# Gate and up of the first layer as seven block products per group of 512 columns

## The reference, cut to what matters

```python
def rms_norm(x, w, eps=1e-6):
    return x * lax.rsqrt(jnp.mean(x * x, axis=-1, keepdims=True) + eps) * w

for l in range(2):
    x = x + mixer[l](rms_norm(x, mix_norm_w[l])) @ w_out[l]
    h = rms_norm(x, ffn_norm_w[l])                    # 512 x 1024
    x = x + (silu(h @ w_gate[l]) * (h @ w_up[l])) @ w_down[l]   # 2816 hidden columns
return rms_norm(x, final_norm_w)
```

## Time and profile before

| | |
|---|---|
| median of the runs | 1233.5 us |
| profiled execution | 1233.71 us, of which the span is 1231.9 us |
| TensorE busy | 1218.4 us, 99% of the span |
| VectorE, ScalarE, POOL busy | 721.6, 515.9, 81.2 us |
| DMA | 122.12 MB, mean 99 GB/s |

### The profile page before, as it was taken

How to read it: one execution, slowest core, us unless ns; L and a number is a source line. 1 busy time by engine, 2 the same in 40 slices (tenths; PEclk the granted TensorE clock), 3 DMA queues, 4 the chain that set the end, 5 groups by cost and what they waited for, 6 DMA issues and landing times.

```text
span 1231.9 us, 16390 instructions
## 1 busy us (share of the span) xinstructions
PE 1218.4 (99%) x5871; PEld 985.6 (80%) x5871; DVE 721.6 (59%) x1176; ACT 515.9 (42%) x845; POOL 81.2 (7%) x179
## 2 busy tenths in 40 slices
PE   9999999999999999999999999999999999999998
PEld 7876658888888888888888888788888888888876
DVE  6787886544444443224777756645565555456796
ACT  6344455432333332123577254445333333224564
POOL 0000000000000000000001734400000000000120
PEclk9999999999999999999999999999999999999999
DMA  7232311332223333222222211011344434436781
GB/s 246 97 117 79 109 49 55 117 103 87 87 99 102 102 101 104 90 97 86 86 90 99 69 50 37 35 52 52 103 133 114 108 98 103 109 102 213 166 151 69
DMA packets 52309, 122.12 MB, mean 99 GB/s; under 512 B 21410, under 2 KB 21666, under 8 KB 52002
## 3 DMA queue, kind: packets, MB, share of 16 engines
q1 hardware_dynamic: 48754, 111.44, 28.6%
q0 software_dynamic: 2592, 8.65, 3.9%
q10 hardware_dynamic: 912, 1.35, 0.4%
HBM read 112.88 MB, written 2.10 MB: 93 GB/s over the span
## 4 chain that ended last, share of the span: by engine, by line
PE 90%; DVE 6%; ACT 2%; issue 1%; ACTq 0%; POOL 0%; DVEq 0%; POOLq 0%
PE PS L1840 89%; DVE wring L1319 1%; PE PS L1916 0%; DVE resid L1323 0%; DVE kept L1359 0%; DVE cacc L1514 0%; ACTq L979 0%; DVE wring L1369 0%; DVE amax L1432 0%; DVE AA L1363 0%; PE PS L2139 0%; ACT wring L792 0%; DVE out L1831 0%; DVE wbuf L1443 0%; DVE hbuf L1639 0%
## 5 line engine op out<-in xcount | busy, mean ns | idle before, releaser
L1840 PE MATMUL PS<-HH,wring 128*128 128x512 f32 x3096 | 723.9, 392 | 0.9 <-DVE vd L1766 0.9
L1840 PEld LDWEIGHTS PS<-HH,wring 128*128 128x128 f32 x3096 | 575.4, 188 | 118.9 <-issue 1.3
L1840 PE MATMUL PS<-AA,wring 128*128 128x512 f32 (+1 forms) x792 | 183.3, 391 | 0.4 <-DVE AA L1448 0.3
L1242 DVE TENSOR_TENSOR wring<-raw,wring 128x1024 fp32r<-128x1024 f32 x108 | 132.0, 1222 | 87.8 <-ACT wring L820 87.6
L1840 PEld LDWEIGHTS PS<-AA,wring 128*128 128x128 f32 x792 | 148.1, 188 | 32.2 <-issue 1.0
L820 ACT ACTIVATE wring<-raw 128x1024 fp32r<-128x1024 f32 x108 | 113.3, 1050 | 109.9 <-PE PS L1840 103.4
L1250 DVE TENSOR_TENSOR ubuf<-PS,rstd 128x512 f32<-128x512 f32 x44 | 30.4, 691 | 183.8 <-PE PS L1840 183.8
L1840 PE MATMUL PS<-wring,AA 128*128 128x512 f32 x462 | 105.4, 389 | 1.6 <-DVE wring L1319 0.8
L1840 PEld LDWEIGHTS PS<-wring,AA 128*128 128x128 f32 x462 | 86.6, 188 | 20.3 <-issue 2.4
L792 ACT ACTIVATE wring<-raw 128x1024 fp32r<-128x1024 f32 x67 | 70.5, 1057 | 76.4 <-PE PS L1840 58.2
L1369 DVE TENSOR_TENSOR wring<-raw,wring 128x1024 fp32r<-128x1024 f32 x67 | 82.5, 1234 | 26.4 <-ACT wring L792 26.4
(11 more groups left out here) (311 smaller groups left out, 1201.3 us busy)
## 6 DMA issues: line engine op xcount, KB each, us to landing
raw<-w_stream SPq DMA_DIRECT2D x171, 512.0 KB, 3.3
kept<-w_last POOLq DMA_DIRECT2D x10, 512.0 KB, 7.6
raw<-w_last SPq DMA_DIRECT2D x5, 512.0 KB, 3.5
kept<-w_last SPq DMA_DIRECT2D x5, 512.0 KB, 6.1
reps<-ub SPq DMA_DIRECT2D x32, 66.5 KB, 2.2
resid<-turned SPq DMA_DIRECT2D x16, 128.0 KB, 5.1
more_first<-w_last SPq DMA_DIRECT2D x1, 1536.0 KB, 12.9
more_first<-w_last POOLq DMA_DIRECT2D x3, 512.0 KB, 5.7
```

The costliest lines, as they stand in the source:

```text
L1242: V.tensor_tensor(wring[:, t % RING, 1], raw[:, t % RAW], wring[:, t % RING, 0].bitcast(f32), ALU.subtract).then_inc(lo_ready[t % RING], 1)
L1840: return nc.tensor.matmul(out, lhsT, rhs, start=start, stop=stop, skip_group_check=adds)
```

## The change

The first two chunks of 128 hidden columns stay as they were: 4 tiles, 96 matmuls (`plain_gate_up`). The other 20 chunks become five groups of 512 columns of gate and 512 of up. A group is a product of two 2x2 block matrices: tokens (two halves of 256) by depth (two halves of 512) on the left, depth by (gate, up) on the right. B11 and B21 are the gate's upper and lower half, B12 and B22 those of up. Seven block products of sums take the place of eight. A block product is 256 tokens by 512 deep by 512 wide, two tiles of 12 matmuls each.

- Left: four sums of token blocks (`diff_full`, `sum_full`, `cross_full`, and the negative of the second depth half, `left_minus`) are made once, from a float32 copy `scaled` of the weighted rows, and split into pairs.
- Right: six of the seven right sides come out of three buffers. `x` holds B11, then B11+B21 (accumulating transfer), then B11+B21+B22 (VectorE, `sum_weights`), then all four (accumulating transfer); `w` holds B21, then B21+B22 (accumulating transfer); `y` holds B22; B12 comes through `raw`. A group is thus 8 plain transfers on SP and 6 accumulating ones on POOL, each of 512 KB. In `wring` a group is 14 tiles of 12 matmuls, where it was 8 tiles of 24.
- Now the tokens are stationary and the weights the moving 512 columns. Results lie with tokens on partitions: 1/rms is a factor per partition (`rtok`), given to Silu as its scale and to VectorE's multiplications. Then TensorE transposes the group's products back, 16 transposes of 128x128 per group (`turn_results`), while the next group runs, and ScalarE copies them out (`keep_turned`).
- `AA` is gone here: the products are kept in float32 (`AF`) and split during `down` (`chunk_high`, `chunk_low`) into four places `AS`. `down` takes its first four tiles two banks at a time.
- TensorE's, VectorE's and ScalarE's loops of the stage are written out.

The diff, cut to its core:

```diff
+G_M11, G_M12, G_M22, G_M21, G_SUM, G_LAST, G_ALL = range(GLU_PRODUCTS)
+GLU_BANK = (0, 2, 0, 2, 4, 0, 2)
+GLU_ADDS = (G_M22, G_M21, G_LAST, G_ALL)
+TURN_BANK = 6
...
+        def load_part(place, sem_at, j, kh, u):
+            for p in range(2):
+                n = sem_at + p
+                if place is w_part and j:
+                    t = glu_tile(j - 1, G_LAST, p)
+                    sp.wait_ge(lo_ready[t % RING], slot_round(t))
+                elif place is y_part and j:
+                    t = glu_tile(j - 1, G_M22, p)
+                    sp.wait_ge(lo_ready[t % RING], slot_round(t))
+                    sp.wait_ge(sem("lhs_made"), weights_summed(j - 1, p))
+                elif place is x_part[j % 2] and j >= 2:
+                    t = glu_tile(j - 2, G_ALL, p)
+                    sp.wait_ge(lo_ready[t % RING], slot_round(t))
+                sp.wait_ge(part_loaded[n], 16 * (j + 1))
+                sp.dma_start(place[:, p], glu_d[j, kh, u][:, p * TILE:(p + 1) * TILE]).then_inc(part_loaded[n], 16)
+        sp.wait_ge(tile_used, T_OUT0 + RING)
...
+        for j in range(GROUPED):
+            for n in range(6):
+                d, p = 6 * j + n, n % 2
+                if n < 2:
+                    t = glu_tile(j, G_M11, p)
+                    pool.wait_ge(lo_ready[t % RING], slot_round(t))
+                    to, addend = x_part[j % 2][:, p], glu_d[j, 1, 0]
+                elif n < 4:
+                    pool.wait_ge(part_loaded[4 + p], 16 * (j + 2))
+                    to, addend = w_part[:, p], glu_d[j, 1, 1]
+                else:
+                    t = glu_tile(j, G_SUM, p)
+                    pool.wait_ge(lo_ready[t % RING], slot_round(t))
+                    to, addend = x_part[j % 2][:, p], glu_d[j, 0, 1]
+                if d >= ADDING:
+                    pool.wait_ge(added[d % ADDING], 16 * (d // ADDING))
+                nc.gpsimd.dma_start(to, addend[:, p * TILE:(p + 1) * TILE], accum_op=ALU.add).then_inc(added[d % ADDING], 16)
...
+        def after_glu_hi(g):
+            j, step = divmod(g, GLU_STEPS)
+            if step == 2 and j:
+                for b in range(2):
+                    act.wait_ge(sem("ffn_mul"), glu_made(j - 1, "gate_first", b))
+                    nc.scalar.activation(gate_first[:, b], gate_first[:, b], ACT.Silu, scale=rtok[:, b:b + 1]).then_inc(sem("gate_silu"), 1)
+            if j < GROUPED and step == 5:
+                act.wait_ge(tile_used, glu_tile(j, G_M11, 1) + 1)
+                if j:
+                    act.wait_ge(sem("ffn_mul"), glu_made(j - 1, "second", 1))
+                for b in range(2):
+                    nc.scalar.activation(glu_q[:, b], PS[:, GLU_BANK[G_M11] + b], ACT.Copy).then_inc(sem("copied"), 1)
+            if j < GROUPED and step == 12:
+                for b in range(2):
+                    act.wait_ge(sem("ffn_mul"), glu_made(j, "gate_second", b))
+                    nc.scalar.activation(glu_q[:, b], glu_q[:, b], ACT.Silu, scale=rtok[:, 2 + b:3 + b]).then_inc(sem("gate_silu"), 1)
+            if j < GROUPED and step == 13:
+                act.wait_ge(tile_used, glu_tile(j, G_SUM, 1) + 1)
+                if j:
+                    act.wait_ge(sem("glu_turned"), 4 * j)
+                for b in range(2):
+                    nc.scalar.activation(glu_s[:, b], PS[:, GLU_BANK[G_SUM] + b], ACT.Copy).then_inc(sem("copied"), 1)
+            if j and step == (7 if j < GROUPED else 3):
+                keep_turned(j - 1, 0)
+            if j and step == (9 if j < GROUPED else 3):
+                keep_turned(j - 1, 2)
+        def keep_turned(j, c0):
+            for c in (c0, c0 + 1):
+                act.wait_ge(sem("glu_turned"), 4 * j + c + 1)
+                nc.scalar.activation(kept_chunk(2 + 4 * j + c), PS[:, TURN_BANK + c % 2], ACT.Copy).then_inc(sem("glu_kept"), 1)
...
+            left_scaled()
+            norm_root(1)
+            nc.scalar.activation(left_minus[:, :, 0], scaled[:, 4:8], ACT.Copy, scale=-1.0).then_inc(sem("ffn_hi"), 1)
+            act.wait_ge(sem("lhs_made"), 1)
+            nc.scalar.activation(left_diff[:, :, 0], diff_full[:], ACT.Copy).then_inc(sem("ffn_hi"), 1)
+            glu_hi(0)
+            glu_hi(1)
+            for c in range(2):
+                act.wait_ge(evacuated, eg + 2 * c + 1)
+                nc.scalar.activation(gate_plain[:, c], gate_plain[:, c], ACT.Silu).then_inc(sem("gate_silu"), 1)
+                glu_hi(2 + c)
+            act.wait_ge(sem("lhs_made"), LEFT_SUMS)
+            act.wait_ge(tile_used, T_GLU)
+            nc.scalar.activation(HH[:, 0:4, 0, 2 * P:S], sum_full[:], ACT.Copy).then_inc(sem("ffn_hi"), 1)
+            nc.scalar.activation(HH[:, 4:8, 0], cross_full[:], ACT.Copy).then_inc(sem("ffn_hi"), 1)
+            for g in range(4, GROUPED * GLU_STEPS):
+                glu_hi(g)
+                after_glu_hi(g)
+                if 0 <= g - (GROUPED * GLU_STEPS - RING) < RING:
+                    chunk_high(g - (GROUPED * GLU_STEPS - RING))
...
+        def left_sums():
+            dve.wait_ge(sem("lhs_scaled"), KD)
+            V.tensor_tensor(diff_full[:], scaled[:, 0:4, 2 * P:S], scaled[:, 4:8, 2 * P:S], ALU.subtract).then_inc(sem("lhs_made"), 1)
+            norm_rstd_tokens(1, PS[:, 7, 0:NB])
...
+        def glu_lo(g):
+            j, step = divmod(g, GLU_STEPS)
+            a, p = divmod(step, 2)
+            t = T_GLU + g
+            dve.wait_ge(hi_ready[t % RING], slot_round(t))
+            V.tensor_tensor(wring[:, t % RING, 1], glu_source(j, a, p), wring[:, t % RING, 0].bitcast(f32), ALU.subtract).then_inc(lo_ready[t % RING], 1)
+        def sum_weights(j, p, addend, sem_at, behind):
+            t = glu_tile(j, behind, p)
+            dve.wait_ge(lo_ready[t % RING], slot_round(t))
+            dve.wait_ge(part_loaded[sem_at + p], 16 * (j + 2))
+            V.tensor_tensor(x_part[j % 2][:, p], x_part[j % 2][:, p], addend[:, p], ALU.add).then_inc(sem("lhs_made"), 1)
+        def glu_results(j, name):
+            bank = {"q": G_M12, "up_first": G_M22, "gate_second": G_M21, "gate_first": G_LAST, "up_second": G_ALL}
+            if name in bank:
+                dve.wait_ge(tile_used, glu_tile(j, bank[name], 1) + 1)
+            for b in range(2):
+                if name == "q":
+                    dve.wait_ge(sem("copied"), 4 * j + b + 1)
+                    ins = V.tensor_tensor(glu_q[:, b], PS[:, GLU_BANK[G_M12] + b], glu_q[:, b], ALU.add)
...
+                elif name == "gate_first":
+                    dve.wait_ge(sem("copied"), 4 * j + 2 + b + 1)
+                    if j:
+                        dve.wait_ge(sem("glu_turned"), 4 * j)
+                    ins = V.tensor_tensor(gate_first[:, b], PS[:, GLU_BANK[G_LAST] + b], glu_s[:, b], ALU.add)
+                elif name == "up_second":
+                    dve.wait_ge(sem("ffn_mul"), glu_made(j, "gate_first", b))
+                    ins = V.tensor_tensor(glu_s[:, b], PS[:, GLU_BANK[G_ALL] + b], glu_s[:, b], ALU.add)
+                elif name == "first":
+                    dve.wait_ge(sem("gate_silu"), 2 + 4 * j + 2 + b + 1)
+                    ins = V.scalar_tensor_tensor(gate_first[:, b], up_first[:, b], rtok[:, b:b + 1], gate_first[:, b], ALU.mult, ALU.mult)
+                else:
+                    dve.wait_ge(sem("gate_silu"), 2 + 4 * j + b + 1)
+                    dve.wait_ge(sem("ffn_mul"), glu_made(j, "up_second", b))
+                    ins = V.scalar_tensor_tensor(glu_s[:, b], glu_s[:, b], rtok[:, 2 + b:3 + b], glu_q[:, b], ALU.mult, ALU.mult)
+                ins.then_inc(sem("ffn_mul"), 1)
+        def after_glu_lo(g):
+            j, step = divmod(g, GLU_STEPS)
+            if j:
+                if step == 1:
+                    glu_results(j - 1, "gate_first")
+                elif step == 3:
+                    glu_results(j - 1, "up_second")
+                    glu_results(j - 1, "first")
+                if step == (4 if j < GROUPED else 3):
+                    glu_results(j - 1, "second")
+            if j < GROUPED:
+                if step == 6:
+                    sum_weights(j, 0, y_part, 2, G_M21)
+                elif step == 7:
+                    glu_results(j, "q")
+                elif step == 8:
+                    sum_weights(j, 1, y_part, 2, G_M21)
+                elif step == 9:
+                    glu_results(j, "up_first")
+                elif step == 11:
+                    glu_results(j, "gate_second")
...
+        def turn_results(j, c0):
+            if j:
+                pe.wait_ge(sem("glu_kept"), 4 * j + c0)
+            else:
+                pe.wait_ge(norm_rstd, 2)
+                if c0:
+                    pe.wait_ge(sem("glu_kept"), c0)
+            pe.wait_ge(sem("ffn_mul"), glu_made(j, "second", 1))
+            for c in (c0, c0 + 1):
+                for b in range(NB):
+                    last = nc.tensor.transpose(PS[:, TURN_BANK + c % 2, blk(b)], glu_result(b)[:, blk(c)], ident)
```

(40 more changed lines are left out.)

375 lines of the change are left out of this document (271 added, 104 removed).

## The result

The changed kernel takes 1217.6 us (median of 4 runs, 1217.1 to 1218.75); the kernel before took 1233.5 us (1233.3 to 1233.6, 4 runs). The ratio is 0.987, 95% interval 0.9855 to 0.989. Forecast were 1218.0 us, range 1214.5 to 1227.

The account below looks back on a forecast made before the run. The prediction took TensorE, without idle time in the stage, as the bound: matmuls times their spacing. Terms -26.9 + 9.8 + 1.3 = -15.8 us; 1233.7 - 15.8 = 1217.9, stated as 1218, range 1214.5 to 1227.

Parts of the forecast that it names:

- Matmuls: Gate and up stage: 960 matmuls go (217.8 us), 840 come (190.9 us), all on the path: -26.9 us.
- Transposes: TensorE, 16 a group, 80 in all: 0.44 us for four, 8.8 us; with the switches +9.8 us on the path.
- switches: TensorE changing between matmuls and transposes: 0.1 us each, ten of them, 1.0 us.
- A steady group: One group of 14 tiles and 16 transposes lasts 40.1 us on TensorE, which waits for nothing; cost 0.
- tight places: Change of group: VectorE and ScalarE finish what the first four products and the transposes need, 2 us or more early.
- Transfers: DMA in each group: plain and accumulating transfers need 30.4 us of the engines in 40.1 us; cost 0.
- slower rival: Accumulating transfers in a group cannot overlap: 7.6 us each, 45.6 us a group, time 1245; chance 0.08, 0.06 of it slower.
- Start: Before the first block product at 247.1: ScalarE's and VectorE's preparation is covered; cost 0, at worst 3 us.
- End: Passage into `down`: TensorE stands still for VectorE's `second` before the last transposes, +1.3 us (ends 0 and 4).
- The sum: Whole kernel: matmuls, transposes with switches, and the wait at the end together give -15.8 us.

## Why the prediction was right, step by step

*Matmuls.* -26.9 forecast. The 40 tiles that went took 241.24 - 23.64 (the four plain tiles with the norm's matmuls, 223.65 to 247.29) = 217.6 us; the sum had 217.8. A new product takes 5.44 us, so 35 take 190.4 where 190.9 stood. The difference is -27.2, and the run with 24 more matmuls a group confirms the price. The spacing, 5.44 / 24 = 0.2267 us, is what the loop had before (0.2269): neither the swapped operands nor the written-out code made a matmul cheaper or dearer.

*Transposes.* Forecast 8.8 and 1.0 for switches. They start 0.10 us apart, 8 us for 80. The 0.1 for a switch holds, but not where the prediction had read it: the product before the transposes keeps its 5.44 us, the one after takes 302.60 - 297.05 = 5.55. Together 9.0, where 9.8 stood; each transpose done twice gave 8.5 for the 80 alone.

*A steady group.* Forecast 40.1 us, no wait; measured 39.9, no wait. The tight places have about the spare time that was worked out for them. In the third group TensorE needs its first two banks at 325.25 and 330.69, begins the transposes at 336.13, and the third and fourth product at 336.93 and 343.29. The timelines of VectorE and ScalarE there:

```profile
322.30 1.28 DVE L1532 TENSOR_TENSOR hbuf<-PS,glu_s 128x512 f32<-128x512 f32 x2
...
327.74 1.28 DVE L1535 TENSOR_TENSOR glu_s<-PS,glu_s 128x512 f32<-128x512 f32 x2
...
332.90 1.09 ACT L994 ACTIVATE glu_q<-PS 128x512 f32<-128x512 f32 x2 [0.89 <-DVE glu_s L1542]
...
338.63 1.28 DVE L1521 TENSOR_TENSOR glu_q<-PS,glu_q 128x512 f32<-128x512 f32 x2
```

`gate_first` is done at 323.6 and `up_second` at 329.0, 1.7 us early each; 2 and 1.9 were forecast. `second` is done at 332.8, 3.3 us before the transposes (3.6 forecast), ScalarE's copies at 334.0, 2.9 before the third product (2.5), and `q` at 339.9, 3.4 before the fourth (4.0). The run with five more operations measured the first of these by itself. VectorE is busy for 27.96 us of a group, forecast 29.4: its operations on two banks come two in 1.28 us, not 0.69 each, and the multiplications two in 1.41, not 0.75 each. ScalarE is busy for 21.19 (22.3).

*Transfers.* DMA share 0.76 in a group; forecast 30.4 of 40.1. The queues in the third group, and landings:

```profile
q0 software_dynamic: 871, 3.17, 45.8%
q1 hardware_dynamic: 1152, 4.19, 29.7%
...
w_part<-w_glu POOLq DMA_DIRECT2D x2, 512.0 KB, 11.2
...
x_odd<-w_glu POOLq DMA_DIRECT2D x2, 512.0 KB, 5.4
```

That is 3.05 us of the engines for an accumulating transfer and 1.48 for a plain one (2.9 and 1.63 forecast). The additions into `w_part` landed after 11.2 us, beyond the 5 to 8 forecast for landings, and had the time. The slower rival named the right mechanism: 45.6 us a group if the six cannot overlap, and 47.0 to 47.6 lay between POOL's first issues of two groups when they were kept from it. Its price was too low in two places. It counted landings alone, so that 6.7 us for each would have been the edge, and with 6.4 the group was long past it: the gaps between issues are a microsecond longer than a landing, and 4.5 us go by between groups. And the low clock behind the waits and a slower passage into `down` came on top, so that the time was 1254.5 and not 1245. It fails here on its condition, as the prediction argued from three transfers in 7.2 us.

*Start.* The first block product came at 247.29; forecast 247.1. Nothing before it waited, cost 0.

*End.* Forecast 1.3 us; measured 1.50, released by `second` of VectorE (`glu_s`, L1542), as the steps had it. `down` takes 123.17 us in place of 119.68 (464.81 to 584.49 before): the wait, 16 transposes and two switches, 3.3, leave 0.2.

*The sum.* Forecast -15.8. At the end of `down` the changed kernel is 584.49 - 568.12 = 16.4 us ahead (its start 0.1 later): the terms missed by -0.3 (matmuls), -0.8 (transposes) and +0.4 (wait and rest of `down`). The medians differ by 15.9. That they agree with the forecast to 0.4 us is in part luck; the terms alone are 0.7 off. The two profiled executions of it differ behind that: one span is 1216.9, the other 1215.7. The difference has a place: the second layer's mixer, from 780 us. The rows are windows of the changed kernel, of the kernel before at the same work, and of the changed kernel's second profile:

```profile
780.00:790.00 10.00, 9.15 (x66) 8.13 (x65) 5.30 (x13) 4.82 (x11) 0.00 (x0) 0.83 0.00 0
```

```profile
796.00:806.00 10.00, 9.15 (x72) 7.68 (x71) 6.40 (x13) 6.00 (x12) 0.34 (x1) 1.00 0.01 2
```

```profile
780.00:790.00 10.00, 9.15 (x71) 7.68 (x70) 6.32 (x13) 6.21 (x13) 0.00 (x0) 1.00 0.01 2
```

The granted clock is 0.83 in the first. The same kernel has it in one execution and not in another, so it is no part of the change.

What was wrong, besides that rival's price, was in expectations after the prediction: the durations of transfers on full engines (eight more), and that one accumulating transfer at a time would do. In the first I had taken a transfer's time at a lighter load as fixed; in the second I had compared engine time (6 x 3 us) with the group and forgotten that a landing takes 6.4 us even when the engines are free.

## What to carry to other kernels

Where TensorE has no idle time in a stage, price a change by matmuls times the spacing of their starts, then walk the ring of slots and list the spare time at each place where another engine must be done; here that came out within 0.6 us at each place, and the only wait stood where the walk put it. For transfers work out two numbers apart: engine time for all of them (here 30 of 40 us, and up to 39.4 cost nothing), and latency divided by how many are in flight (6.4 us each, fatal with one, hidden with two). A wait at a passage between stages is first a matter of order: 12 matmuls moved ahead of it removed it.
